# Expert weights of a retrieval layer: the slot's gate and diagonal made by VectorE in one operation, gelu once for two slots

## The reference

```python
q = (tc @ wq).reshape(PEER_CHUNK, PEER_HEADS, 2, PEER_QDIM // 2)
s = jnp.einsum('thpd,hpkd->thpk', q, keys)
sv, si = lax.top_k(s, PEER_TOPK)          # 16 best of 128, per head and side
...                                       # 16 best sums of the 256 pairs -> e, top_s
g = jax.nn.softmax(top_s, axis=-1)
act = jax.nn.gelu(jnp.einsum('thkd,td->thk', u[e], tc), approximate=False)
return jnp.einsum('thk,thkd->td', g * act, v[e])
```

## Time and profile before

| | |
|---|---|
| median of 3 runs | 3155.49 us (3150.79 to 3157.68) |
| the profiled execution | 3152.39 us |
| its span | 3150.6 us |
| PE (TensorE) busy | 2350.4 us, 75% |
| DVE (VectorE) busy | 1899.9 us, 60% |
| ACT (ScalarE) busy | 1267.1 us, 40% |
| POOL (GpSimd) busy | 883.8 us, 28% |
| DMA moved | 1011.35 MB, 321 GB/s over the span |
| L2345, a dot product | 1225 ns, 768 times |
| L1563, L1565, L1570 on ScalarE | 200, 294 and 348 ns, 768 times each |
| L1187 on TensorE, a pair of slots | 8 records of 784 ns on average, 384 pairs |

### The profile page before, as it was taken

The page is one execution under the profiler, slowest core; times in us unless marked ns, Lnnn a source line. Parts: engine busy times, 40 slices in busy tenths (PEclk is TensorE's granted clock), DMA queues, the critical chain, the costliest instruction groups (busy, mean ns, idle before and its releaser), DMA issues.

```text
span 3150.6 us, 33641 instructions
## 1 busy us (share of the span) xinstructions
PE 2350.4 (75%) x11532; PEld 1360.1 (43%) x11532; DVE 1899.9 (60%) x4493; ACT 1267.1 (40%) x3385; POOL 883.8 (28%) x790
## 2 busy tenths in 40 slices
PE   5998998686689979666556788768998855555555
PEld 3787897243246645221212344227797611111111
DVE  3328646876665554686667544446854796666654
ACT  4216535345643333343333433244644534333333
POOL 0000000433243333333334343310000244444442
PEclk8999998887789999887867898869998977787777
DMA  5631344999899999999999999953143699999996
GB/s 235 249 126 34 108 161 146 422 378 378 312 370 402 401 421 413 408 405 421 405 421 398 417 421 421 422 219 119 31 178 123 258 418 421 422 421 421 420 419 277
DMA packets 139706, 1011.35 MB, mean 321 GB/s; under 512 B 15632, under 2 KB 15760, under 8 KB 17168
## 3 DMA queue, kind: packets, MB, share of 16 engines
q0 software_dynamic: 112032, 810.08, 62.9%
q1 hardware_dynamic: 27216, 196.45, 16.1%
q10 hardware_dynamic: 288, 2.69, 0.2%
HBM read 1008.10 MB, written 1.05 MB: 320 GB/s over the span
## 4 chain that ended last, share of the span: by engine, by line
PE 42%; DMA 30%; DVE 14%; ACT 8%; issue 3%; POOL 3%; ACTq 0%; POOLq 0%; DVEq 0%; SPq 0%
DMA att<-experts_in,att 28%; PE ps L1187 11%; DVE att L2345 5%; PE ps L602 5%; PE ps L603 5%; PE ps L604 5%; PE ps L1082 4%; POOL att L1761 3%; DVE ring_lo L1807 2%; ACT wt_hi L1283 2%; PE ps L887 2%; PE ps L1132 1%; PE ps L984 1%; PE ps L650 1%; ACT att L1570 1%
## 5 line engine op out<-in xcount | busy, mean ns | idle before, releaser
L1187 PE MATMUL ps<-att 128*64 128x512 f32 x3072 | 996.9, 784 | 674.4 <-ACT att L1570 669.1
L1761 POOL DMA_INDIRECT att<-experts_in,att x768 | 873.4, 1137 | 1794.3 <-PE ps L1187 1140.0
L2345 DVE CUSTOM_DVE_ANT_0 att<-att 128x1024 f32<-128x1024 f32 x768 | 931.8, 1225 | 621.0 <-DMA att<-experts_in,att 616.6
L1187 PEld LDWEIGHTS ps<-att 128*64 128x64 f32 x3072 | 227.5, 165 | 1331.3 <-ACT att L1570 979.6
L1563 ACT ACTIVATE att<-att 128x1 f32<-128x1 f32 x768 | 153.7, 200 | 939.2 <-DVE att L2345 922.5
L1807 DVE TENSOR_TENSOR ring_lo<-ring,wt_hi 128x2048 fp32r<-128x2048 f32 x84 | 192.4, 2292 | 290.2 <-ACT wt_hi L1283 290.1
L1570 ACT ACTIVATE att<-const,att 128x64 f32<-128x64 f32 x768 | 267.1, 348 | 72.0 <-ACT att L1565 1.9
L1565 ACT ACTIVATE att<-att 128x1 f32<-128x1 f32 x768 | 226.2, 294 | 24.9
L1283 ACT ACTIVATE wt_hi<-ring 128x2048 fp32r<-128x2048 f32 x84 | 160.3, 1909 | 175.5 <-PE ps L604 102.9
L602 PE MATMUL ps<-h,wt_hi 128*128 128x256 f32 (+1 forms) x616 | 196.3, 319 | 28.4 <-DVE h L1821 22.0
L603 PE MATMUL ps<-h,wt_hi 128*128 128x256 f32 (+1 forms) x616 | 188.7, 306 | 0.0
(11 more groups left out here) (239 smaller groups left out, 3519.2 us busy)
## 6 DMA issues: line engine op xcount, KB each, us to landing
ring<-stream_in SPq DMA_DIRECT2D x183, 1024.0 KB
att<-experts_in,att POOLq DMA_INDIRECT x768
att<-bias_in POOLq DMA_DIRECT2D x16, 256.0 KB, 2.9
x<-x_in ACTq DMA_DIRECT2D x1, 2048.0 KB, 8.5
att<-stream_in SPq DMA_DIRECT2D x2, 1024.0 KB
spare<-stream_in SPq DMA_DIRECT2D x1, 1024.0 KB
out<-att SPq DMA_DIRECT2D x1, 1024.0 KB, 3.9
const<-const_in ACTq DMA_DIRECT2D x1, 576.0 KB, 4.7
```

The source lines that it names most:

```text
L1187: last = mm(ps[HALF * s:HALF * (s + 1), d, :], diag[:, (m + s) % DIAGS, :], rows[:, (m + s) % SLOTS, D + 512 * d:D + 512 * (d + 1)], start ...
L1761: nc.gpsimd.indirect_dma_start(out=rows[:, m % SLOTS, :], out_offset=None, in_=experts_in, in_offset=bass.IndirectOffsetOnAxis(ap=index[:, ...
L2345: v.tensor_tensor_reduce(out=u_row, in0=u_row, in1=dup[:, n // HK, n % 2, :], scale=1.0, scalar=0.0, op0=ALU.mult, op1=ALU.add, accum_out= ...
```

## The change

ScalarE takes gelu of two columns at once, at odd slots, and nothing more. VectorE, at odd slots, right behind the second dot and ahead of the interleaved work, waits for that gelu, for the gates and for the diagonals' ring, and then makes both diagonals: `fold` times the column of gelu times the column of gates, in one operation each. The semaphore `weight_ready` goes; `diag_ready` is raised by 2 for a pair. TensorE and GpSimd are unchanged, and so is the order of all other work.

```diff
@@ ScalarE, gather @@
                 for n in range(PICKS):
                     m, tt = r * PICKS + n, n // HK
-                    if n % QUARTER == 0:
-                        act.wait_ge(picks_ready, QUARTERS * r + n // QUARTER + 1)
-                    act.wait_ge(dot_done, m + 1)
-                    nc.scalar.activation(acts[:, n:n + 1], dots[:, n:n + 1], ACT.Gelu).then_inc(gelu_done, 1)
-                    act.wait_ge(gelu_done, m + 1)
-                    nc.scalar.activation(acts[:, n:n + 1], acts[:, n:n + 1], ACT.Copy, scale=gates[:, r % 2, n:n + 1])\
-                        .then_inc(weight_ready, 1)
-                    if m >= DIAGS:
-                        act.wait_ge(row_used, (m - DIAGS) // 2 + 1)
-                    act.wait_ge(weight_ready, m + 1)
-                    nc.scalar.activation(diag[:, m % DIAGS, :], fold, ACT.Copy, scale=acts[:, n:n + 1])\
-                        .then_inc(diag_ready, 1)
+                    if n % 2:
+                        act.wait_ge(dot_done, m + 1)
+                        nc.scalar.activation(acts[:, n - 1:n + 1], dots[:, n - 1:n + 1], ACT.Gelu).then_inc(gelu_done, 1)
@@ VectorE, gather, behind the dot product @@
+                    if n % 2:
+                        dve.wait_ge(gelu_done, m // 2 + 1)
+                        dve.wait_ge(picks_ready, QUARTERS * r + n // QUARTER + 1)
+                        if m >= DIAGS:
+                            dve.wait_ge(row_used, (m - DIAGS) // 2 + 1)
+                        for s in range(2):
+                            k = n - 1 + s
+                            last = v.tensor_scalar(diag[:, (m - 1 + s) % DIAGS, :], fold, acts[:, k:k + 1],
+                                                   gates[:, r % 2, k:k + 1], ALU.mult, ALU.mult)
+                        last.then_inc(diag_ready, 2)
```

More of the change, by code:

```diff
@@ L463, in build @@
         gelu_done = sem("gelu_done")
-        weight_ready = sem("weight_ready")
         diag_ready = sem("diag_ready")
```

## The result

The changed kernel took 3162.04 us (median of 18 runs, 3155.79 to 3168.38), the kernel before 3153.62 in the same comparison (18 runs, 3146.49 to 3159.25): ratio 1.0028, 95% interval 1.0019 to 1.0038, so 6 to 12 us slower, 8.8 by the ratio. The forecast was +11, 3164.

What follows compares the result with a forecast made beforehand. No single engine bounds the kernel; time moves only where DMA runs dry. Searches +8.5, +9.4 and +3.2, attention -8.2, holes -1.8, last pair -0.1 sum to +11.0 us: 3164, range 3146 to 3182.

Steps and rivals of the forecast that it cites:

- the forecast case: Whole kernel: VectorE's added work in the searches outweighs attention's gain, 3158 to 3172 us; chance 0.45.
- the merge and the full stretch: 920 to 1090 us, TensorE busy throughout, and 2600 to 3120 us, DMA full: no change in either.
- The price of a pair: VectorE at each odd slot: accumulator read, wait for gelu and two diagonals add 0.92 us, ends 0.66 and 1.3.
- the 0.12 for two satisfied waits: VectorE, between gelu's wait and the first diagonal: two more waits cost some 0.06 us each.
- Searches: 583 to 650 and 2513 to 2577 us, bound by VectorE: 11 and 12 pairs cost +8.5 and +9.4 us.
- The two holes: Short DMA holes, as at 1517 us, where ScalarE sits behind TensorE: first pair ready 0.9 us earlier, -1.8 in all.
- Attention: Context attention, 743 to 896 us: eleven turns each 0.93 us shorter, 10.2, less 2 for searches: -8.2 us.
- rival 2: Context attention: shorter waits may keep TensorE at 2.4 GHz, 1.8 us more saved per turn, net -9 us; chance 0.04.
- The search at the end of pass 0: 1312 to 1341 us, bound by VectorE: 5.5 pairs cost +5.1, less about 1.9, giving +3.2 us.
- the relief of 1.9: 1312 to 1341 us: ScalarE no longer owes two slots of weights behind each of two token copies, about 1.9 us less.
- rival 3: VectorE's stall is longer, 0.41 us operations and waiting behind ScalarE's squares and table loads: 3178 us; chance 0.14.
- rival 4: GpSimd's gather descriptors wait behind VectorE's diagonals, +18 us in starved stretches: 3182 us; chance 0.04.

Runs made afterwards that it cites:

- experiment 5: New form in pass 2 alone, with VectorE making each pair of diagonals twice, against the kernel before: 3170.90 us, ratio 1.0072.
- experiment 2: New form in the 256 slots of pass 2 alone, against the kernel before: 3162.94 us, ratio 1.0034.
- experiment 6: ScalarE's form everywhere, VectorE only waiting for gelu behind each odd slot's dot in pass 2, against the kernel before: 3159.04 us, ratio 1.0026.
- experiment 11: New form in slots 58 to 115 of pass 0 alone, diagonals made twice there, against the kernel before: 3159.38 us, ratio 1.0022.

## Why the prediction was right

**The place and the sign held.** It was the forecast case: VectorE's searches bound, attention gained, the merge and the full stretch stood still (170 us with TensorE busy 168.7; 419 GB/s). That the sum came so near is in part luck: in the order of the table the trace of the changed kernel has +6.2, -10.4, +2.4, +2.2, +5.5, +1.2, +9.4 and +0.9 us beside the trace before, where +8.5, -8.2, 0, 0, +3.2, -1.8, +9.4 and -0.1 were forecast, and misses of 2 us and more stand on both sides.

**The price of a pair** was set at 0.92 us and measured at 0.77 to 0.80. The operations (0.22 each, forecast; 0.42 to 0.45 a pair) and gelu's 0.27 with its signals were right; the 0.12 for two satisfied waits was not: from gelu's end (2567.06) to the first diagonal (2567.10) are 0.04 us, the signal alone. Two take 0.54 us together, by the forecast 0.55. The 0.86 us from read to TensorE's load (forecast 1.00, before 1.06) is smaller for the same reason.

**Searches**: +8.5 forecast in pass 0, +6 to +7 measured (slots 0 to 58); +9.4 in pass 2, +8.7 on the mean of the old traces, +10.7 timed. In pass 2 the lower price is made up for by more turns: the eight pairs read above cost 6.2 us, and pairs just outside the rest (slots 524 to 530 went from 4.93 us a pair to 5.31). In pass 0 slots 34 to 58 gave 1.6 us back. The two holes (-1.8) can't be told from the scatter of pass 1 (744 to 751 us over traces of the same form).

**Attention**: -8.2 forecast; -10 in slots 66 to 116, -8 to the end of slot 200, -5.4 timed by itself. The size was right and half the reason wrong. I wrote "the turns shrink from 13.7 to 12.8 us" by shortening the chain alone, and gave TensorE's clock, as rival 2, a chance of 0.04 and all eleven turns or none. The chain alone gives 0.3 to 0.5 a turn; the rest came from turns in which the clock was granted, 1.9 to 3.6 us for the waiting pair instead of 3.68.

**The search at the end of pass 0** (1312 to 1341 us before, slots 242 to 252): +3.2 forecast, 5.1 for 5.5 pairs less 1.9 because ScalarE owes less behind its copies of tokens. Slots 242 to 256 took 36.5 us in each of the three traces with the new form there and 30.8 to 32.5 in the others: +5.2 on the mean of the old ones, and seven pairs at 0.77 are 5.4. The price is there and the relief of 1.9 is not: in the kernel before, VectorE stands 6.42 us ahead of this search for TensorE, not for ScalarE. So the forecast's term was 2 us too small here. The kernel before, then the changed one, slots 242 to 256:

```profile
1312.39 0.89 DVE L2109 MAX8 att<-ps 128x8 f32<-128x128 f32 x4 [6.42 <-PE ps L969]
...
1314.50:1345.50 31.00, 15.85 (x44) 3.80 (x46) 30.16 (x95) 13.78 (x42) 12.77 (x9) 0.73 0.94 377
...
1315.85:1352.36 36.51, 18.91 (x48) 4.18 (x48) 33.75 (x109) 4.22 (x10) 11.67 (x10) 0.61 0.87 331
```

**VectorE behind ScalarE's queue.** Behind slot 203 ScalarE's queue has an item for the query projection ahead of gelu, and that waits for TensorE. The changed kernel at 1190 to 1198 us, first ScalarE, then VectorE:

```profile
1196.73 0.38 ACT L1525 ACTIVATE att<-ps 128x256 f32<-128x256 f32 x1 [8.96 <-PE ps L1131]
1197.01 0.20 ACT L1561 ACTIVATE att<-att 128x2 f32<-128x2 f32 x1
...
1197.24 0.54 DVE L2345 TENSOR_SCALAR att<-const,att 128x64 f32<-128x64 f32 x2 [6.61 <-ACT att L1561]
```

Before, VectorE went on with three more dot products here (1190.61, 1192.28 and 1196.34 us). Now it stands 6.61 us, since it waits for ScalarE, which waits for TensorE. I had named that ("VectorE waiting behind ScalarE") only within rival 3. It costs nothing in the end: slots 200 to 242 take 128.2 to 130.7 us with the new form and 128.5 to 131.6 with the old.

**Descriptors behind the diagonals** (rival 4, after "SBUF — State Buffer", section "SBUF: two separate sides", of the Trainium skill): the gathers took 1127 ns with 768 more two-scalar operations on VectorE and 1137 without, and 1143 in experiment 5, with 512 of them in pass 2 alone, where the full stretch kept its length; experiment 2, with 256, has 1125, so this is scatter. No run here shows the delay.

**Better than both** are the three kernels with the new form only beside attention: 0.9983, 0.9981 and 0.9981 of the kernel before, which can't be told from each other.

## What to carry to other kernels

Moving work to an engine costs nothing where transfers bound (here 0.77 us a pair, even 1.25) and its full price, waiting included, where that engine's own turn is the longest: choose the form stretch by stretch. When a saving on a chain lies ahead of matmuls that run at the low clock, expect it to be partly given back or to be multiplied by the clock, and bound it both ways. A new wait makes an engine stand behind everything that is queued ahead of the awaited instruction, so look what that queue is waiting for, and then whether the time is lost at all: the 6.6 us of standing here were made up for before slot 242.

## What the runs showed of the hardware

- Two satisfied semaphore waits on VectorE ahead of a two-scalar operation cost nothing visible: gelu's end to the operation's start is 0.04 us, with the wait for gelu and two more between (2567.06 to 2567.10 us in the changed kernel).
- Whether the waiting pair in attention ran at 1.2 or 2.4 GHz was not decided by the idle time directly ahead of it (3.70 us with 1.94, 3.71 with 3.68); over slots 66 to 116 the mean clock went roughly with the length of the chain: 0.75 or 0.76 in six of the seven traces with ScalarE's form, where these waits are 4.1 to 4.9 us in most turns (0.78 in the seventh, experiment 6), 0.77 with mostly 4.15 (experiment 11), 0.80 to 0.84 with 3.7 in most turns.
